# Stick-breaking attention: the weighted sum of values as products of high and low parts

## The reference, cut to what matters

```python
def stick_breaking_attention(q, k, v):
    # A[t,s] = beta[t,s] * prod_{s<j<t} (1 - beta[t,j]) for s < t
    z = einsum('bqhd,bkhd->bhqk', q, k) * HEAD_DIM ** -0.5
    mask = kpos[None, :] < qpos[:, None]
    log_beta = log_sigmoid(z)
    log_1m = where(mask, log_sigmoid(-z), 0.0)
    after = cumsum(log_1m, reverse=True) - log_1m
    a = where(mask, exp(log_beta + after), 0.0)
    return einsum('bhqk,bkhd->bqhd', a, v)
```

## Time and profile before

| what | value |
|---|---|
| median of the runs | 1725.2 us |
| the profiled execution, its time | 1726.02 us |
| its span | 1724.2 us |
| TensorE busy | 1710.1 us |
| VectorE busy | 1044.7 us |
| GpSimd busy | 725.9 us |
| ScalarE busy | 640.2 us |

### The profile page before, as it was taken

One profiled execution on the slowest core, in us unless ns is written; L12 is line 12 of the kernel. 1 busy time (PEld: TensorE's weight loads), 2 busy tenths in 40 slices (PEclk: granted clock), 3 DMA queues, 4 the chain that ended last, 5 costly groups with the idle time before them and its releaser, 6 DMA issues.

```text
span 1724.2 us, 21381 instructions
## 1 busy us (share of the span) xinstructions
PE 1710.1 (99%) x7744; PEld 1399.5 (81%) x7744; DVE 1044.7 (61%) x1217; ACT 640.2 (37%) x891; POOL 725.9 (42%) x307
## 2 busy tenths in 40 slices
PE   8999999999999999999999999999999999999999
PEld 6887888887788888888888888888877778888887
DVE  5766567766665456457674557785544753869441
ACT  5222322225655656221322322213445644333321
POOL 2444344444433431344444444444355433444443
PEclk9999999999999999999999999999999999999999
DMA  5333222325211221243423232323242014222243
GB/s 187 104 107 101 89 98 96 105 90 181 86 62 62 88 72 37 73 135 98 138 98 111 85 110 98 102 98 104 94 166 74 25 37 171 97 90 97 97 141 116
DMA packets 44992, 173.14 MB, mean 100 GB/s; under 512 B 5065, under 2 KB 5193, under 8 KB 44140
## 3 DMA queue, kind: packets, MB, share of 16 engines
q1 hardware_dynamic: 39312, 150.23, 26.2%
q10 hardware_dynamic: 5596, 21.73, 3.6%
HBM read 161.32 MB, written 10.62 MB: 100 GB/s over the span
## 4 chain that ended last, share of the span: by engine, by line
PE 94%; issue 3%; POOL 1%; ACT 1%; DVE 1%; DMA 0%; POOLq 0%; SPq 0%; DVEq 0%; ACTq 0%
PE psum L305 28%; PE psum L307 28%; PE psum L306 28%; PE psum L1685 2%; POOL wlo L271 1%; PE psum L1156 1%; PE psum L1169 1%; PE psum L1674 1%; PE psum L711 0%; PE psum L696 0%; PE psum L907 0%; PE psum L682 0%; PE psum L1146 0%; PE psum L1646 0%; DMA xT<-x_dram 0%
## 5 line engine op out<-in xcount | busy, mean ns | idle before, releaser
L271 POOL TENSOR_TENSOR wlo<-raw,whi 128x1024 fp32r<-128x1024 f32 (+2 forms) x262 | 673.6, 2571 | 911.3 <-ACT whi L293 910.7
L293 ACT ACTIVATE whi<-raw 128x1024 fp32r<-128x1024 f32 (+2 forms) x263 | 290.3, 1104 | 727.4 <-PE psum L307 720.4
L305 PE MATMUL psum<-h_hi,whi 128*128 128x512 f32 x1360 | 538.3, 396 | 0.2 <-DVE h_lo L387 0.2
L307 PE MATMUL psum<-h_hi,wlo 128*128 128x512 f32 x1360 | 530.1, 390 | 0.0
L306 PE MATMUL psum<-h_lo,whi 128*128 128x512 f32 x1360 | 530.0, 390 | 0.0
L305 PEld LDWEIGHTS psum<-h_hi,whi 128*128 128x128 f32 x1360 | 255.7, 188 | 57.6 <-issue 4.2
L306 PEld LDWEIGHTS psum<-h_lo,whi 128*128 128x128 f32 x1360 | 255.7, 188 | 55.3 <-issue 3.4
L307 PEld LDWEIGHTS psum<-h_hi,wlo 128*128 128x128 f32 x1360 | 255.6, 188 | 53.5
L305 PE MATMUL psum<-mid_hi,whi 128*128 128x512 f32 x352 | 137.2, 390 | 0.0
L307 PE MATMUL psum<-mid_hi,wlo 128*128 128x512 f32 x352 | 137.0, 389 | 0.0
L306 PE MATMUL psum<-mid_lo,whi 128*128 128x512 f32 x352 | 136.9, 389 | 0.0
(11 more groups left out here) (369 smaller groups left out, 2462.8 us busy)
## 6 DMA issues: line engine op xcount, KB each, us to landing
raw<-wk_dram SPq DMA_DIRECT2D x224, 512.0 KB, 3.7
raw<-wd_dram SPq DMA_DIRECT2D x32, 704.0 KB, 4.0
raw<-wp_dram SPq DMA_DIRECT2D x8, 640.0 KB, 3.8
spectra_scratch<-spec_out ACTq DMA_DIRECT2D x8, 512.0 KB, 3.8
x_scratch<-xT ACTq DMA_DIRECT2D x2, 2048.0 KB, 7.4
xT<-x_scratch ACTq DMA_DIRECT2D x8, 512.0 KB, 4.4
spec<-spectra_scratch ACTq DMA_DIRECT2D x2, 2048.0 KB, 10.3
xT<-x_dram SPq DMA_DIRECT2D x4, 512.0 KB, 7.7
```

The source lines that it names most:

```text
L271: pool.tensor_tensor(wlo[s][:, 0:w], raw[s][:, 0:w], whi[s][:, 0:w].bitcast(F32), ALU.subtract).then_inc(lo_ready, 1)
L293: act.activation(whi[s][:, 0:w], raw[s][:, 0:w], ACT.Copy).then_inc(hi_ready, 1)
L305: pe.matmul(dst, s_hi, m_hi, start=start and i == 0, stop=False, **kw)
L307: last = pe.matmul(dst, s_lo, m_hi, start=False, stop=stop and i == n - 1, **kw)
```

## The change

The last product of the stick-breaking attention is made of parts. The values are stored as `sv_hi` (float32r, in the place of `v32s`) and as low parts, which lie in unused columns: those of value block s, 384 columns, behind column 1024 of `whi0`, `whi1`, `wlo0` or `wlo1`, and the other 128 columns behind column 1024 of `raw0` or `raw1`. VectorE makes the low parts, in two pieces for each block. The weights' high parts go into the buffers of queries and keys of heads 0 and 1, which are spent by then: four ScalarE copies for each head, after the exponential. The low parts overwrite the float32 weights: four GpSimd subtractions for each head. GpSimd's splitting of weight units in this stage is put between them in a fixed order. The outputs wait for the low parts, and use three matmuls for each block in place of one. The semaphore of the rotary tables is merged with another one; the number of semaphores stays the same.

```diff
-        v32s = at(80, "v32s", [P, TT, T])
+        sv_hi = at(80, "sv_hi", [P, TT, T], F32R)
+        raw_rest = [nc.alloc_sbuf_tensor_at(f"raw_rest{s}", [P, 3 * P], F32R, offset=raw0 + (s * FH * P + D) * 4)
+                    for s in range(2)]
+        weight_lo = [at(103, "weight_lo0", [P, AREA_COLS], F32R),
+                     nc.alloc_sbuf_tensor_at("weight_lo1", [P, AREA_COLS], F32R, offset=scratch0 + 3 * T * 4)]
...
-                    act.activation(v32s[:, t, :], bank(4 + t), ACT.Copy).then_inc(self.v, 1)
+                    act.activation(sv_hi[:, t, :], bank(4 + t), ACT.Copy).then_inc(self.v, 1)
...
+            def weight_hi(self, h, s):
+                n, e = T - s * P, h % 2
+                spent, a = ((sq_hi, 0), (sq_lo, 0), (sk_both, 0), (sk_both, 2 * P))[s]
+                return spent[:, e, a:a + n]
+            def value_lo(self, s, p):
+                if p < 3:
+                    return (*whi, *wlo)[s][:, D + p * P:D + (p + 1) * P]
+                return raw_rest[s // 3][:, (s % 3) * P:(s % 3 + 1) * P]
+            def values_lo(self, s):
+                return ((*whi, *wlo)[s][:, D:D + 3 * P], self.value_lo(s, 3))
...
             def tensor_z(self, pe, h):
                 if h >= 2:
-                    pe.wait_ge(self.weight, h - 1)
+                    pe.wait_ge(self.weight, 2 * h - 3)
...
             def tensor_outputs(self, pe, h):
-                pe.wait_ge(self.weight, h + 1)
+                pe.wait_ge(self.weight_lo, h + 1)
...
-                    last = pe.matmul(psum[:, 512 * 6 + s * P:512 * 7], v32s[:, s, (h // 2) * P:(h // 2 + 1) * P],
-                                     weight[h % 2][:, AREA[s]:AREA[s] + T - s * P], start=s == 0, stop=s == TT - 1)
+                    last = products(pe, psum[:, 512 * 6 + s * P:512 * 7],
+                                    [(sv_hi[:, s, (h // 2) * P:(h // 2 + 1) * P], self.value_lo(s, h // 2),
+                                      self.weight_hi(h, s), weight_lo[h % 2][:, AREA[s]:AREA[s] + T - s * P])],
+                                    start=s == 0, stop=s == TT - 1)
...
-                pe.wait_ge(stickp.v, 2)
+                pe.wait_ge(stickp.v, 4)
...
                 act.activation(weight[h % 2][:, :], self.whole(h), ACT.Exp).then_inc(self.weight, 1)
+                act.wait_ge(self.weight, 2 * h + 1)
+                for s in range(TT):
+                    last = act.activation(self.weight_hi(h, s), weight[h % 2][:, AREA[s]:AREA[s] + T - s * P], ACT.Copy)
+                last.then_inc(self.weight, 1)
+            def pool_weight_lo(self, pool, h):
+                pool.wait_ge(self.weight, 2 * h + 2)
+                for s in range(TT):
+                    zone = slice(AREA[s], AREA[s] + T - s * P)
+                    last = pool.tensor_tensor(weight_lo[h % 2][:, zone], weight[h % 2][:, zone],
+                                              self.weight_hi(h, s).bitcast(F32), ALU.subtract)
+                last.then_inc(self.weight_lo, 1)
+            def pool(self, pool):
+                u = BASE["part1"]
+                for h in range(HEADS):
+                    self.pool_weight_lo(pool, h)
+                    if h in (0, 1, 3, 5):
+                        n = (2, 3, 0, 4, 0, 5)[h]
+                        stream_lo(pool, u + n, u + n + 1)
...
-                    pe.wait_ge(self.seven_read, 10 + b)
+                    pe.wait_ge(self.seven_read, 11 + 2 * b)
...
+            def vector_values_lo(self, dve, t):
+                for dst, (a, b) in zip(stick.values_lo(t), ((0, 3 * P), (3 * P, T))):
+                    last = dve.tensor_tensor(dst, bank(4 + t)[:, a:b], sv_hi[:, t, a:b].bitcast(F32), ALU.subtract)
+                return last
             def vector_values(self, dve):
+                dve.wait_ge(stickp.v, 2)
+                for t in (0, 1):
+                    self.vector_values_lo(dve, t).then_inc(stickp.v, 1)
                 dve.wait_ge(unit_done, BASE["sb_v"] + 4)
                 for t in (3, 2):
-                    dve.tensor_copy(v32s[:, t, :], bank(4 + t)).then_inc(self.seven_read, 1)
+                    dve.tensor_copy(sv_hi[:, t, :], bank(4 + t)).then_inc(self.seven_read, 1)
+                    dve.wait_ge(self.seven_read, 16 - 2 * t)
+                    self.vector_values_lo(dve, t).then_inc(self.seven_read, 1)
...
-                act.dma_start(rope[:, :], rope_in).then_inc(rope_landed, 16)
+                act.dma_start(rope[:, :], rope_in).then_inc(const_landed, 16)
...
-            stream_lo(pool, BASE["sb_q"] + 4, BASE["mla_z"])
+            stream_lo(pool, BASE["sb_q"] + 4, BASE["part1"] + 2)
+            stick.pool(pool)
+            stream_lo(pool, BASE["part1"] + 6, BASE["mla_z"])
```

More of the change, by code:

```diff
@@ L114, in build @@
         raw = [keep(f"raw{s}", [P, FH * P]) for s in range(2)]
+        raw0 = nc.sbuf_base - 2 * FH * P * 4
         vec = keep("vec", [P, VEC_COLS])
@@ L350, in build @@
         const_landed = sem("const_landed")
-        rope_landed = sem("rope_landed")
         constr_ready = sem("constr_ready")
@@ L1127, in __init__ @@
                 (self.z, self.az, self.e, self.l, self.sp, self.masked, self.hi, self.ready, self.sums, self.weight,
-                 self.outputs, self.out_hi, self.out) = (
+                 self.weight_lo, self.outputs, self.out_hi, self.out) = (
                     sem(f"stick_{x}") for x in ("z", "abs", "exp", "ln", "softplus", "masked", "sp_hi", "sp_ready",
-                                                "sums", "weight", "outputs", "out_hi", "out"))
+                                                "sums", "weight", "weight_lo", "outputs", "out_hi", "out"))
+            def weight_hi(self, h, s):
[8 more added lines that the diff above has]
+                return ((*whi, *wlo)[s][:, D:D + 3 * P], self.value_lo(s, 3))
             def zone(self, h, s, a=0, n=None):
@@ L1564, in load @@
                 act.wait_ge(filters.stored, 80)
-                act.dma_start(rope[:, :], rope_in).then_inc(rope_landed, 16)
+                act.dma_start(rope[:, :], rope_in).then_inc(const_landed, 16)
                 for a, b, n in ((0, 96, 32), (32, 64, 32), (64, 0, 64)):
-                    act.dma_start(rope_odd[a:a + n, :], rope_in[b:b + n, :]).then_inc(rope_landed, 16)
+                    act.dma_start(rope_odd[a:a + n, :], rope_in[b:b + n, :]).then_inc(const_landed, 16)
             def tensor_latents(self, pe):
@@ L1912, in vector_latents @@
                 low, high = slice(HD, QKD), slice(QKD, P)
-                dve.wait_ge(rope_landed, 64)
+                dve.wait_ge(const_landed, 112)
                 dve.tensor_scalar(tab_q[:, :], rope[:, :], col("g_qn"), QKD ** -0.5, ALU.mult,
```

## The result

The changed kernel takes 1730.53 us (median of ten runs, 1729.29 to 1730.63); the kernel before took 1725.61 beside it (ten runs). The ratio is 1.0026, 95% interval 1.0018 to 1.0034: slower, by 4.9 us. The profiled execution took 1730.47 with a span of 1728.7, 4.5 more than before.

The account below looks back on a forecast made before the run. TensorE was taken to bound the kernel, busy 1710.1 of 1724.2 us. The terms −2.2 + 1.3 + 2.5 + 2.7 = +4.3 us gave 1729.5 us, range 1726.0 to 1732.0.

Parts of the forecast that it names:

- TensorE's work: Stick-breaking outputs: 1.89 us per head, 0.24 less, plus 0.04 from following logits in six rounds; 2.2 us less in all.
- first stall: Start of the stage: GpSimd runs between VectorE's masks, so branch part 3 waits for part 1's product; 1.3 us.
- sums of head 7: TensorE waits 2.9 us for sp_lo, against 0.4 to 0.5 before, with GpSimd going between sp_hi and sp_lo; 2.5 more.
- last head: Last outputs wait for copies and low weights with no round to hide in; 2.7 us, ends 1.9 and 4.0.
- the case without GpSimd in between: Rival at both meeting places: GpSimd and VectorE just miss; head 7 costs 1.2, total +1.7, 1726.9 us; chance 0.22.
- the delay is passed on whole and not added to: Behind the stage: TensorE never waits for the merge's first ScalarE or VectorE operations, covered by eight gate chunks, 5.4 us.
- What was costed at nothing: Value lows run free on VectorE, middle rounds hide copies and lows, the merged rope semaphore moves no transfer; no cost.

Follow-up runs that it names:

- experiment 1: The kernel before with only the new twelve-matmul outputs, no real low parts, copies, subtractions or waits (result not right): 1724.36 us, ratio 0.9990.
- experiment 5: The changed kernel with ScalarE's split of the third part unit moved from behind softplus 1 to behind softplus 2: 1728.12 us, ratio to before 1.0014.
- experiment 2: The kernel before with the merged rope semaphore, its last outputs waiting for three idle GpSimd subtractions: 1726.91 us, ratio 1.0006.
- experiment 3: The kernel before with the merged rope semaphore, its last outputs waiting for four idle GpSimd subtractions: 1729.43 us, ratio 1.0022.
- experiment 4: The changed kernel with four chunks of the next gate unit (12 matmuls) moved ahead of the last head's outputs: 1725.94 us, ratio to before 1.0000.
- Experiment 8: The changed kernel with one signal per ScalarE weight copy, each GpSimd subtraction waiting for its own copy only: 1730.47 us, ratio to before 1.0028.
- experiment 7: The changed kernel with four gate chunks ahead of the last outputs and the third part and second gate unit splits moved later: 1724.07 us, ratio to before 0.9987.
- experiment 6: The changed kernel with the second gate unit's split moved behind round 7's weights, its subtraction behind head 6's lows: 1728.44 us, ratio to before 1.0013.

## Why the prediction was right, and where it was wrong

The predicted 1729.5 lies 1.0 below the measured 1730.53, and the direction and the main cause stand: TensorE's work got shorter, three waits cost more. The terms, in the stage:

| step | foreseen | measured | from |
|---|---|---|---|
| TensorE's work | −2.2 | −1.9 | a round 0.25 less; experiment 1: −1.8 with a wait of 0.3 |
| first stall | +1.3 | +1.04 | 642.79 − 641.47, less 0.28 of a later stage; experiment 5: 1.04 |
| sums of head 7 | +2.5 | +1.0 | 0.16 ahead of before at the gate matmul (689.76), 0.82 behind at the sums (692.47) |
| last head | +2.7 | +2.4 | 702.23 against 699.79, where the chunks end |
| clock | 0 | +1.6 | 9.07 against 7.5 |
| sum | +4.3 | +4.2 | stage 107.37 against 103.18 |

So that the sum came out is in part luck: two errors of about 1.5 have opposite signs, head 7, seen in the trace of after, and the clock, shown by experiments 2 to 4. Of the 4.3 foreseen, the terms that were named give 2.5.

**The gain.** The way of reading the price of a matmul from the starts of its neighbours held: 1.92 for the outputs against 1.89.

**The start.** The masks were cut apart as foreseen, 3.11 us (the like stood at 611.69 in the earlier trace rows). Only the term was some 0.3 smaller. The product of part 1 ended at 636.74, as foreseen (636.8), but part 3 was due later: the whole stage began 0.28 later. The prediction's own two times, 636.8 and 635.6, also give 1.2 and not 1.3.

**Head 7** is the step that failed. The prediction has "it goes between sp_hi and sp_lo, for 1.3". In the profile GpSimd and VectorE asked within 0.01 us, and VectorE won:

```profile
690.93 1.49 DVE L1305 TENSOR_TENSOR sp_lo<-scratch,sp_hi 128x1280 fp32r<-128x1280 f32 x1
```

```profile
690.94 2.62 POOL L1243 TENSOR_TENSOR weight_lo<-weight,sq_hi 128x512 fp32r<-128x512 f32 x1 [2.72 <-ACT sk_both L1236]
```

Counted from the end of the sums of head 5 (679.38), GpSimd asked at 11.56, where 11.6 was foreseen, but VectorE had ended sp_hi at 11.52 and not at 11.8. So its chain was 0.3 earlier than worked out, sp_lo came first, GpSimd waited 1.3 (2.62 for a subtraction of 1.30), and TensorE did not pay. What is left, 1.0, is near the 1.2 that the prediction gave for the case without GpSimd in between. Experiment 8 shows that the mechanism itself was right: a GpSimd that asks 0.03 before sp_hi costs TensorE 1.8 more (2.90 against 1.13). A term that hangs on who comes first by 0.1 us should have stood at half its price.

**The last head.** Copies in 1.55 (697.20 to 698.75), lows in 3.4. The rows behind it, ScalarE and then GpSimd:

```profile
697.20 0.63 ACT L1236 ACTIVATE sq_hi<-scratch 128x512 fp32r<-128x512 f32 x1
```

```profile
698.83 1.29 POOL L1243 TENSOR_TENSOR weight_lo<-scratch,sq_hi 128x512 fp32r<-128x512 f32 x1 [3.18 <-ACT sk_both L1236]
700.08 1.00 POOL L1243 TENSOR_TENSOR weight_lo<-scratch,sq_lo 128x384 fp32r<-128x384 f32 x1
701.04 1.14 POOL L1243 TENSOR_TENSOR weight_lo<-scratch,sk_both 128x256 fp32r<-128x256 f32 x2
```

**The clock** was not in the prediction at all. It took the price of a stall to be its length; experiments 2, 3 and 4 show that a stall of 0.9 is priced so, and that one of 2.2 to 2.3 costs 1.6 to 1.7 more when the clock falls behind it. The sentence "TensorE is never waiting ... so the delay is passed on whole and not added to" is the wrong one: there is no new wait in the gate behind the last outputs, but its matmuls ran at the low clock and added to the delay.

What was costed at nothing cost nothing: the value lows ran free of GpSimd at 0.75 us a tile, the middle rounds hid copies and lows, and the merged semaphore moved nothing that shows (the 1017.4 us behind the stage are the same).

**Left open.** Ten runs of the changed kernel fall into seven of 1730.47 to 1730.63 and three of 1729.29 to 1729.64. The clock holding in the shorter runs would be of this size, but so would a shorter slow stretch at the start of the program. The runs of experiment 7, without a stall that could bring the clock down, fall apart in the same way: five of 1723.03 to 1723.36 and six of 1724.07 to 1724.78. There is no trace of a run of the shorter kind, so neither is shown.

## What to carry to other kernels

Where one engine is busy 99% of the time, a change that shortens its work by moving some to others pays only if the last item of the pipeline has cover too: in the steady rounds 5 us of new work on ScalarE and GpSimd was free, and at the last head half of it was a stall, until 12 matmuls that were needed anyway were put in front. Look for neighbours between GpSimd and SBUF-only VectorE instructions on the path and keep them apart by more than the error of your working. And price a stall of TensorE of the length seen here, 2.2 us or more, at more than its length: in four of five profiled executions with such a stall the clock fell behind it, for 1.6 us or more on top.

## What the runs showed of the hardware

- The float32 product of 128 x 128 with 1280 columns took 2.13 us; three float32r products of the same took 1.92.
- The granted clock fell from 1.00 to 0.50, the 1.2 GHz level, after, not during, a TensorE stall of 2.2 to 2.3 us (the changed kernel, experiments 3 and 5), and came back about 3 us later. Behind the stall of 2.90 in experiment 8 it stayed low for more than 6 us. Behind a stall of 0.94 the mean granted clock of the program was 1.000 in all eleven runs; behind stalls of 1.1 the clock held in three profiled executions (changed, experiments 4 and 5). It also held behind 2.28 in the profiled execution of experiment 6. The Trainium skill (TensorE: Matmul & The Clock Gate, Part 1: The HAM clock gate) says that the window in which activity is watched runs free of the kernel, so that the point of change varies from run to run. The two outcomes behind 2.28 agree with that, and so does the change of pace at the start of the program, at 14.09 in one execution and 11.02 in another, but no trace here shows the window.
- GpSimd subtractions and VectorE instructions with SBUF operands alone took turns by whole instructions in both directions: each waited for the other's current one (1.30 became 2.62; 0.83 became 1.94). VectorE's operations on PSUM (0.56 for 384 columns beside a subtraction) were not held. The Trainium skill (GPSIMD Engine Reference, section 8, Key points) names contention with VectorE instructions that have two SBUF inputs or run in a 2-port mode. The rows agree for those of two inputs (the masks, sp_lo) and show a wait for a whole instruction; sp_hi, of one input, waited too, and no row shows its mode.
